# Two more places in the ring of expert weights, filled ahead and copied by GpSimd

## The reference, cut to what matters

```python
def moe(h, w_router, b_router, w_gate, b_gate, w_up, b_up, w_down, b_down):
    logits = t @ w_router + b_router
    top_v, top_e = lax.top_k(logits, TOP_K)            # 4 of 32 experts for each token
    gates = jax.nn.softmax(top_v, axis=-1)
    ...
    def block_step(out, inp):                           # one block of rows of one expert e
        xb = t[toks]
        a = jnp.minimum(xb @ w_gate[e] + b_gate[e], SWIGLU_LIMIT)
        b = jnp.clip(xb @ w_up[e] + b_up[e], -SWIGLU_LIMIT, SWIGLU_LIMIT)
        hid = a * jax.nn.sigmoid(SWIGLU_ALPHA * a) * (b + 1)
        y = hid @ w_down[e] + b_down[e]
        return out.at[toks].add(y * gw[:, None]), None
```

## Time and profile before

| what | us |
|---|---|
| median of 3 runs | 1535.19 (1534.07 to 1537.6) |
| the profiled execution's own time | 1529.43 |
| its span in the trace | 1527.6 |
| PE busy, whole span | 1293.0 |
| DVE busy, whole span | 490.8 |
| POOL busy, whole span | 120.4 |
| mean granted clock of TensorE | 0.923 |

### The profile page before, as it was taken

How to read it: one execution, slowest core, us unless ns; L and a number is a source line. 1 busy time by engine, 2 the same in 40 slices (tenths; PEclk the granted TensorE clock), 3 DMA queues, 4 the chain that set the end, 5 groups by cost and what they waited for, 6 DMA issues and landing times.

```text
span 1527.6 us, 27237 instructions
## 1 busy us (share of the span) xinstructions
PE 1293.0 (85%) x11224; PEld 598.6 (39%) x11225; DVE 490.8 (32%) x1015; ACT 259.3 (17%) x480; POOL 120.4 (8%) x160
## 2 busy tenths in 40 slices
PE   4899899645768479999889889888899999999995
PEld 0746333445654333343333333333333343333432
DVE  0116333563478562221221122121222232221323
ACT  2411421203411311111111111110001010010102
POOL 1101221243241300000000000000000000000000
PEclk9599999955789679999999999999999999999998
DMA  9303356000013569999999999999999699988993
GB/s 363 164 0 102 146 191 226 12 3 32 5 36 111 226 262 428 427 428 427 428 429 427 428 429 427 427 426 429 425 427 429 268 430 427 427 348 356 428 428 134
DMA packets 46948, 456.99 MB, mean 299 GB/s; under 512 B 4227, under 2 KB 4483, under 8 KB 21795
## 3 DMA queue, kind: packets, MB, share of 16 engines
q1 hardware_dynamic: 46886, 456.08, 71.9%
HBM read 455.01 MB, written 1.05 MB: 299 GB/s over the span
## 4 chain that ended last, share of the span: by engine, by line
PE 34%; DMA 27%; DVE 2%; ACT 2%; issue 1%; DVEq 0%; ACTq 0%
DMA arena<-in_w_up 27%; PE bank L1043 20%; PE bank L1072 8%; PE bank L1015 2%; PE bank L1006 2%; ACT arena L1368 1%; PE bank L1036 1%; PE bank L1067 0%; DVE arena L1854 0%; ACT arena L1366 0%; DVE arena L1857 0%; ACT L1121 0%; ACT L1119 0%; DVE arena L1998 0%; DVE arena L1848 0%
## 5 line engine op out<-in xcount | busy, mean ns | idle before, releaser
L1043 PE MATMUL bank<-arena 128*64 128x512 f32 x2176 | 483.3, 597 | 34.8 <-DMA arena<-in_w_up 19.4
L1043 PEld LDWEIGHTS bank<-arena 128*64 128x64 f32 x2176 | 154.8, 137 | 344.7 <-issue 268.5
L1072 PE MATMUL bank<-arena 128*64 128x512 f32 x1088 | 239.4, 592 | 0.0
L1962 DVE TENSOR_SCALAR arena<-bank 128x512 f32<-128x512 f32 x34 | 23.6, 693 | 393.4 <-PE bank L1043 393.4
L1072 PEld LDWEIGHTS bank<-arena 128*64 128x64 f32 x1088 | 78.5, 136 | 138.1 <-issue 135.8
L573 PE MATMUL bank<-arena 128*128 128x512 f32 (+1 forms) x320 | 119.0, 528 | 0.0
L1943 DVE TENSOR_TENSOR arena<-arena,bank 128x512 f32<-128x512 f32 x140 | 86.6, 682 | 6.0 <-PE bank L1015 6.0
L573 PEld LDWEIGHTS bank<-arena 128*128 128x128 f32 x320 | 60.2, 189 | 55.9 <-issue 53.5
L1006 PEld LDWEIGHTS bank<-arena 128*128 128x128 bf16 x1680 | 60.3, 118 | 27.0 <-DVE arena L1966 25.8
L1015 PE MATMUL bank<-arena 64*128 64x512 f32 x280 | 69.6, 614 | 0.9 <-ACT arena L1370 0.9
L1006 PE MATMUL bank<-arena 128*128 128x64 bf16 x1680 | 64.1, 199 | 1.1 <-DVE arena L1885 1.1
(11 more groups left out here) (332 smaller groups left out, 1150.1 us busy)
## 6 DMA issues: line engine op xcount, KB each, us to landing
arena<-in_w_gate SPq DMA_DIRECT2D x64, 2048.0 KB, 20.9
arena<-in_w_up SPq DMA_DIRECT2D x64, 2048.0 KB, 22.6
arena<-in_w_down SPq DMA_DIRECT2D x64, 2048.0 KB, 21.4
arena<-in_w_ada SPq DMA_DIRECT2D x12, 2048.0 KB, 9.4
arena<-in_wfm SPq DMA_DIRECT2D x20, 512.0 KB, 6.8
arena<-in_wz SPq DMA_DIRECT2D x2, 2048.0 KB, 20.5
arena<-in_w_out SPq DMA_DIRECT2D x1, 4096.0 KB, 14.6
arena<-in_x SPq DMA_DIRECT2D x2, 1024.0 KB, 11.0
```

The source lines that it names most:

```text
L1043: last = mm(ps[m][64 * c_:64 * c_ + 64, :], xcT[:, k, :], ring[:, 2 * h_ + m, k % 4, 512 * c_:512 * c_ + 512], start=False, stop=(k == KT ...
L1072: last = mm(ps[2][64 * c_:64 * c_ + 64, :], hidT[:, k % 4, 64 * (k // 4):64 * (k // 4) + 64], ring[:, 4 + h_, k % 4, 512 * c_:512 * c_ + 5 ...
L1962: v.tensor_scalar(hid[:, 0], ps[0][:, :], LIMIT, None, ALU.min).then_inc(*L.mark("a"))
```

## The change

The ring gets eight places. The pieces 0 and 1 of expert 0 still go to places 0 and 1. For every later expert SP puts them into places 6 and 7, and GpSimd copies them (L2223 of the new code, one copy of 128 x 4096 floats for each) to places 0 and 1, where PE reads them. Three waits change with it:

- SP issues pieces 0 and 1 of expert e once GpSimd has copied those of e-1 (`held0`, `held1`), no longer once PE has finished with them. For pieces 2 to 5 the wait is the one of before.
- GpSimd copies piece n of e once it has landed and PE has finished with piece n of e-1.
- PE waits for `held0` and `held1` instead of `in_ring0` and `in_ring1`.

Places 6 and 7 lie over buffers of the router (`h`, `hT`), so SP waits for the router's last readers before its loop. Other buffers move: `acc` lies over the rows of weights that the router has used, so that GpSimd clears it after its part of `hparts` and not before; `passed` moves to `hid`; the result is written to `xin`.

```diff
-            def pieces(blocks, expert):
-                L.begin_turn(blocks)
-                for n, (m, c) in enumerate(order):
-
+            def load_piece(n, place, expert):
+
+                m, c = order[n]
+                src = halves[m][bass.ds(expert, 1), c].rearrange("e p n -> p (e n)")
+                sp.dma_start(ring[:, place].rearrange("p k n -> p (k n)"), src).then_inc(sems(f"in_ring{n}"), 16)
+
+            def pieces(expert):
+
+                for n in range(2):
+                    sp.wait_ge(sems(f"held{n}"), expert)
+                    load_piece(n, PIECES + n, expert)
+                L.begin_turn(sp.value_load(intab[0:1, bass.ds(expert + (BLOCKS - 1), 1)], min_val=1, max_val=BLOCKS - 1))
+                for n in range(2, PIECES):
                     sp.wait_ge(*L.at("pe", "piece", n))
-                    src = halves[m][bass.ds(expert, 1), c].rearrange("e p n -> p (e n)")
-                    sp.dma_start(ring[:, n].rearrange("p k n -> p (k n)"), src).then_inc(sems(f"in_ring{n}"), 16)
-
-            pieces(0, 0)
-            L.turn = None
+                    load_piece(n, n, expert)
+                L.turn = None
+
+            for n in range(PIECES):
+                load_piece(n, n, 0)
+            sp.wait_ge(*L.at("pe", "logit", 1))
+            sp.wait_ge(*L.at("dve", "hparts"))
+            sp.wait_ge(*L.at("pool", "hparts"))
             sp.wait_ge(*L.at("dve", "table"))
             with sp.Fori(1, E_N) as i:
-                pieces(sp.value_load(intab[0:1, bass.ds(i + (BLOCKS - 1), 1)], min_val=1, max_val=BLOCKS - 1), i)
+                pieces(i)
...
                     for m in range(2):
-                        pe.wait_ge(sems(f"in_ring{2 * h_ + m}"), expert * 16 + 16)
+                        if h_:
+                            pe.wait_ge(sems(f"in_ring{2 * h_ + m}"), expert * 16 + 16)
+                        else:
+                            pe.wait_ge(sems(f"held{m}"), expert + 1)
...
+            dve.wait_ge(*L.at("pool", "hparts"))
             v.tensor_tensor(passed, cum.unsqueeze(1).broadcast_to([P, BLOCKS, 32]),
...
             L.stage("route")
-            g_.memset(acc.rearrange("p a b -> p (a b)"), 0.0).then_inc(*L.mark())
-
             pool.wait_ge(*L.at("dve", "h", 1))
...
+            g_.memset(acc.rearrange("p a b -> p (a b)"), 0.0).then_inc(*L.mark())
             pool.wait_ge(*L.at("pe", "logit", 1))
             g_.memset(GT.rearrange("p a b -> p (a b)"), 0.0).then_inc(*L.mark())
             g_.memset(ysb, 0.0).then_inc(*L.mark("zeros"))
+
+            L.stage("moe")
+            for n in range(2):
+                pool.wait_ge(sems(f"in_ring{n}"), 16)
+                pool.sem_inc(sems(f"held{n}"), 1)
+            pool.wait_ge(*L.at("dve", "table"))
+            with pool.Fori(1, E_N) as i:
+                L.begin_turn(pool.value_load(intab[0:1, bass.ds(i + (BLOCKS - 1), 1)], min_val=1, max_val=BLOCKS - 1))
+                for n in range(2):
+                    pool.wait_ge(sems(f"in_ring{n}"), i * 16 + 16)
+                    pool.wait_ge(*L.at("pe", "piece", n))
+                    pool.sem_inc(sems("passing"), 1)
+                    g_.tensor_copy(ring[:, n].rearrange("p k n -> p (k n)"),
+                                   ring[:, PIECES + n].rearrange("p k n -> p (k n)")).then_inc(sems(f"held{n}"), 1)
```

More of the change, by code:

```diff
@@ L43 @@
 PIECES = 6
+SLOTS = PIECES + 2
 FM = ([("k", i, True) for i in range(4)] + [("q", i, False) for i in range(4)]
@@ L173, in lay_out_sbuf @@
     put(keep, ("bstage", 3 * D))
-    e = put(keep, ("h", 2 * D), ("hp", 3 * D), ("wr", 256), ("bias", 3 * 512), ("acc", 2 * D), ("hid", 6 * 512))
-    assert at["bstage"][0] + 3 * D <= at["bT"][0] and at["wr"][0] >= at["k_tm"][0]
-    assert at["bias"][0] + at["bias"][1] <= at["xs_tm"][0]
-    put(e, ("hT", KT * 256))
-    e = put(e, ("xcT", 512), ("hidT", 512), ("y", 512), ("GT", 256), ("Sg", 256))
-    put(e, ("Sb", 64), ("route", 1500), ("ring", PIECES * 4096))
+    e = put(keep, ("hp", 3 * D), ("bias", 3 * 512), ("hid", 6 * 512))
+    assert at["bias"][0] >= at["bstage"][0] + 3 * D and at["hid"][0] >= at["k_tm"][0]
+    put(e, ("ring", SLOTS * 4096))
+    put(e + PIECES * 4096, ("h", 2 * D), ("hT", KT * 256))
+    put(CONSTS["tri"][0], ("GT", 256), ("Sg", 256), ("Sb", 64), ("route", 1500), ("wr", 256))
+    assert at["wr"][0] + 256 <= CONSTS["m1t"][0] + 256
+    put(at["rows"][0], ("acc", 2 * D))
+    put(at["gates"][0] + 128, ("xcT", 512), ("hidT", 512), ("y", 512))
     return at
@@ L318, in layer_program @@
         Sb = area("Sb").bitcast(BF16).rearrange("p (t s) -> p t s", t=2)
-        ring = view(area("ring"), PIECES, 4, D)
+        ring = view(area("ring"), SLOTS, 4, D)
         r_at = [0]
@@ L350, in layer_program @@
         gsel = route(2, 1)
-        passed = view(area("rows", 0, BLOCKS * 32), BLOCKS, 32)
+        passed = view(area("hid", 0, BLOCKS * 32), BLOCKS, 32)
         selb = route(32).bitcast(BF16)
@@ L1853, in _ @@
                 dve.wait_ge(*L.own())
-                v.tensor_copy(hparts[:, s_, 0], hm[:, 0] if s_ == 0 else x1[:, 0]).then_inc(*L.mark())
+                v.tensor_copy(hparts[:, s_, 0], hm[:, 0] if s_ == 0 else x1[:, 0]).then_inc(*L.mark("hparts"))
                 if s_ < 2:
@@ L1999, in _ @@
                 dve.wait_ge(*L.own())
-                v.tensor_tensor(hm[:, t], acc[:, t], xin[:, t], ALU.add).then_inc(*L.mark("out", t))
+                v.tensor_tensor(xin[:, t], acc[:, t], xin[:, t], ALU.add).then_inc(*L.mark("out", t))
         @block.gpsimd
```

3 lines of the change are left out of this document (1 added, 2 removed).

## The result

| | before | after |
|---|---|---|
| median of 4 runs, us | 1535.13 (1534.07 to 1537.60) | 1551.46 (1546.40 to 1552.62) |
| the profiled execution's own time, us | 1529.43 | 1552.62 |
| its span, us | 1527.6 | 1550.8 |
| PE's first piece of expert 0, us | 551.0 | 559.3 |
| the mixture: from there to PE's first piece of expert 31, us | 931.3 | 946.3 |

A forecast was written before the change was run, and what follows sets the result against it. The weights' transfers bound the kernel, except around three stops, where PE limits. PE 0.8 us later at expert 27, plus a 1.65 us collision behind the third stop, made +2.45 us: median 1537.6 us, range 1534 to 1547.

The forecast's parts named there:

- the drift: In blocks behind a stop: next landing 29.4 us later, PE's block after 28.3, so the copy comes 1.1 us later.
- rival 2: In PE's blocks: a copy above 4.2 us keeps meeting DVE, stream in step with PE; about +125 us, chance 0.08.
- The stream's gain: At the stops of the weights' transfers: piece 4 starts earlier, by 0.8 us at the start and 0.4 later.
- The copy at 3.6 us: On GpSimd: each copy of 128 x 4096 floats takes 3.6 us, between bounds of 3.1 and 9.5.
- The lag of the copies: Where the transfers limit: PE runs 0.6 us later against the stream, counted once when PE takes over as limit.
- The lock of two engines for whole instructions: In PE's blocks: GpSimd's copy and DVE's two-input SBUF instructions wait for each other; L1061 starts 1.65 us later.
- Rival 4: At the copies: DVE's two-input instructions don't wait for GpSimd; +0.3 us at most, chance 0.52 together with the forecast.
- Behind the second stop: After the stop at expert 22's second block, where PE limits: one collision of copy and DVE, +1.65 us.
- Behind the third stop: After the stop at expert 27's second block, PE limiting to the end: one collision, +1.65 us.
- Behind the start: After the mixture's first stop: the same collision, but the transfers limit again and hide it.
- Edits at nothing: Moved memset of `acc`, `passed`, SP's new waits, first `held` counts: no cost, at most 1.8 us once.
- Rival 1: Behind each stop: collisions in more than one block, or copies of 4 to 5 us; +4 to +10 us, chance 0.32.

The follow-up runs named there:

- e4: The changed kernel measured once more, nothing altered; 1547.38 us, ratio 1.0087 to the kernel before.
- e1: The changed kernel without GpSimd's copies, GpSimd only counting, PE reading expert 0's first two pieces in every block; 1533.05 us, ratio 1.0008 to the kernel before.
- e2: The changed kernel with DVE's steps L1984, L1986 and L1989 kept in bank 1, none with two SBUF inputs; 1535.04 us, ratio 1.0003 to the kernel before.
- e3: The changed kernel with GpSimd's copies also waiting until DVE has made `hid` in the block before; 1535.39 us, ratio 1.0010 to the kernel before.
- e5: The changed kernel with each copy cut into four of 128 x 1024 floats; 1535.44 us, ratio 1.0001 to the kernel before.
- e10: The kernel of e3 with the memset of `acc` moved behind PE's first gather; 1533.70 us without one run of 1718.22, ratio 0.9992 to the kernel before.

## Why the prediction was wrong

**The step that failed** is the one that set the collisions to one block behind each stop: "The next landing lies 29.4 us later, while PE's block came after 28.3, [...] and from there on the two part." In the run PE's block came after 31.6 us and the landing after 31.3. Three things were missing. The first is a term: with a collision the granted clock of PE fell to 0.5 in five of the nine blocks that had a full one (in three of six in e4), at 1.5 to 2.7 us each in the first profile. The second is a size: the holes themselves cost 2.26 us in expert 23's block and not 1.65, so that even without the low clock this block would have been 28.9 us (31.58 less 2.68, an estimate) and the drift 0.5 us and not 1.1. The third is what a block above 29.4 us does: it makes PE the limit of the stream again at piece 4, so the landing moves along with PE and nothing drifts. The collision keeps itself up by that, as rival 2 said of a dearer copy. The sum counted the drift in full, though I had put the margin at 0.4 us myself. The experiments carry the collision's part (e1, e2, e3 and e5 each take the collisions away and end at 928.2 to 930.6 us, and in none of the four does the clock fall in the mixture but at the skipped turns, as in the kernel before). That the low clock itself sets the run of collisions was not tried apart: expert 24's block, without it, still led to another collision, so it is shown as a cost (4.4 us behind the second stop) and only argued as the reason for their number.

Term by term:
- The stream's gain, 0.8 us at the start and 0.4 at later stops: right in kind, with pieces 4 and 5 holding the stream as forecast, but too small. In e1 the prefetch gives 3.1 us of the mixture, 0.75 of it in the first block.
- The copy at 3.6 us: 3617 ns, median 3605. The dense rows were the right ones to stand on.
- The lag of the copies where the transfers limit, 0.6 us: the place is right (PE waits 25.3 us in all for L2223), the size too small. With e2 and e3 at 930.3 and 930.0 us, against 928.2 without copies, it is about 2 us with all that hangs on it. The larger gain and the larger lag nearly cancel, which is luck: e2 and e3, without the collisions, end 1.0 and 1.3 us below the kernel before.
- The lock of two engines for whole instructions: right, in size and place. The first collision came at L1986 of expert 23 with 0.02 us between the starts (forecast 0.4), and 1.79 us of wait at L1080; L1080 began 1.94 us later in its block than undisturbed (19.59 us behind the block's first piece against 17.65), where 1.65 was forecast. Rival 4 (no lock) is out. The Trainium skill's rule (SBUF — State Buffer, Who interferes with whom) names two-input instructions of VectorE, and the run agrees for those: 4.14 against 0.69 us. The same section says that an instruction with at most one SBUF input, outside the modes that take both ports, doesn't contend; e2 agrees for L1986 and L1989, with 0.70 and 0.69 us under a copy.
- Behind the second stop I had one collision, +1.65: measured +11.5 in four blocks, holes 7.98, low clock 4.38, less 0.87 given back by the transfer at expert 27, which I had foreseen as 0.8.
- Behind the third stop +1.65: measured +1.99, one collision, and none after it. Here the step held.
- Behind the start "the transfers limit again and hide it": right for the most part. 12.3 us of delay shrink to 1.5; against e2, which has the copies and no collisions, 2.8 us are left.
- Edits at nothing: false for the memset of `acc`. I had looked at what it must be ready for, not at whom it runs beside; 1.25 us, within the 1.8 that the prediction named as the most. I had also looked for the lock at two-input instructions alone. The Trainium skill's SBUF — State Buffer (Who interferes with whom) names tensor_scalar too, where it runs in a mode that takes both ports; L1890's 1.35 us agrees. `passed` and SP's waits cost nothing that can be seen.

Rival 1 (several collisions behind each stop, +4 to +10 us, chance 0.32) is what happened, beyond its top, since it had no clock term and ended each chain at two. The sum as measured: +15.0 (12.2 in e4) in the mixture and +1.25 ahead of it make 13.4 to 16.3 us; the medians differ by 16.3, and the ratio's interval is 9.1 to 19.5 us.

## What to carry to other kernels

When a helper engine's long instruction may land beside another engine's critical one, ask first whether the coincidence is tied to the same event on both sides: if the delay it causes moves both, it recurs and is paid per turn, not once. Part them by a wait, by an operand in a bank, or by cutting the long instruction to less than the slack; each removed the whole loss here. And see which piece really holds a stream before giving places to another: two places for pieces 0 and 1 alone brought about 1 us, which is not told from nothing; the same two places open to all pieces, with a loop that skips no turns, brought 10 to 13.

## What the hardware showed that I had not expected

- A memset on GpSimd, which reads nothing, holds up DVE's instructions from SBUF to SBUF with one input: 1.35 us instead of 0.23 to 0.33 for 4 floats a partition (L1890, after and e10).
- Such instructions wait for a GpSimd copy too: L1971 took up to 3.73 us in e2 and 3.72 in e3, at a mean of 344 ns without copies (e1). The instructions that read a bank (L1982, L1984, L1963) kept their 0.67 to 0.70 us in all kernels.
- A hole of 1.79 us in PE's work was followed by 6.8 us at half the clock, with the block's usual hole of 0.8 us coming just after the fall. The length of the hole doesn't decide it: in e4 one of 1.32 us was followed by 3.4 us at half the clock, while 1.75 and 1.76 us in the blocks of experts 26 and 28 were followed by none. What decides it stays open.
- The loop over further blocks costs PE time: where 13 turns are skipped, the gap is 7.3 us beyond the usual one with one body inside; with four bodies the three gaps at that loop are 46.8 us, and in one loop with its end read from the table they are gone. How much of the 46.8 is skipping and how much the change of bodies isn't shown.
